# Head of a hybrid layer kernel: the first modulation by single channel blocks, with the products of the high parts first

## The reference, cut to what matters

```python
c_act = silu(c)
mod = c_act @ w_mod + b_mod              # six vectors of 1024
sh_m, sc_m, gt_m, sh_f, sc_f, gt_f = split(mod, 6)
h = rms_norm(x, g_pre_mix) * (1.0 + sc_m) + sh_m
proj = h @ w_in                          # 7 x 1024 columns
b_a, c_a, v_a, x_b, g_b, u_a, u_b = split(proj)
y_a = b_a * conv3(c_a * v_a)
x_b = conv4(x_b)
y_b = rg_lru(x_b) * gelu(g_b)            # two block-diagonal gates, a scan
...                                      # merge, output projection, MLP
```

## Time and profile before

| | us |
|---|---|
| median of 3 runs (lowest to highest) | 826.84 (826.39 to 827.14) |
| the profiled execution | 826.06 |
| its span, first to last instruction | 824.2 |
| TensorE busy | 815.0 (99%) |
| VectorE, ScalarE, GpSimd busy | 507.1, 440.4, 29.1 |

### The profile page before, as it was taken

One profiled execution on the slowest core, in us unless ns is written; L12 is line 12 of the kernel. 1 busy time (PEld: TensorE's weight loads), 2 busy tenths in 40 slices (PEclk: granted clock), 3 DMA queues, 4 the chain that ended last, 5 costly groups with the idle time before them and its releaser, 6 DMA issues.

```text
span 824.2 us, 12511 instructions
## 1 busy us (share of the span) xinstructions
PE 815.0 (99%) x4292; PEld 704.3 (85%) x4292; DVE 507.1 (62%) x672; ACT 440.4 (53%) x655; POOL 29.1 (4%) x30
## 2 busy tenths in 40 slices
PE   8999999999999999999999999999999999999997
PEld 8887888888888888888888899999999888888885
DVE  4776666665585655665784688777776533333335
ACT  6557777776664443444243657666676632233332
POOL 1640000000000000000000000000000000000000
PEclk8999999999999999999999999999999999999999
DMA  9951433326096666676437031333333423322302
GB/s 320 348 159 33 118 109 108 107 78 182 26 271 190 201 188 178 193 204 178 128 127 231 1 103 52 103 102 102 103 109 119 155 103 102 99 82 99 102 1 102
DMA packets 132895, 109.52 MB, mean 133 GB/s; under 512 B 4460, under 2 KB 117252, under 8 KB 132868
## 3 DMA queue, kind: packets, MB, share of 16 engines
q1 hardware_dynamic: 132772, 109.12, 44.3%
q10 hardware_dynamic: 64, 0.02, 0.0%
q0 software_dynamic: 32, 0.02, 0.0%
HBM read 107.04 MB, written 2.10 MB: 132 GB/s over the span
## 4 chain that ended last, share of the span: by engine, by line
PE 94%; DVE 2%; ACT 1%; DMA 1%; issue 1%; SPq 0%; ACTq 0%; DVEq 0%
PE ps L438 31%; PE ps L439 30%; PE ps L440 30%; PE ps L1488 1%; DMA graw<-in_w_gate_i_dram 1%; PE ps L1509 0%; DMA erows<-in_b_mod_dram 0%; PE ps L1653 0%; PE ps L1496 0%; DVE sp L1075 0%; PE ps L1522 0%; DVE w_lo L1143 0%; PE ps L1625 0%; PE ps L1626 0%; PE ps L1535 0%
## 5 line engine op out<-in xcount | busy, mean ns | idle before, releaser
L438 PE MATMUL ps<-ht_hi,w_hi 128*128 128x512 f32 x448 | 175.5, 392 | 0.0
L439 PE MATMUL ps<-ht_lo,w_hi 128*128 128x512 f32 x448 | 174.7, 390 | 0.0
L440 PE MATMUL ps<-ht_hi,w_lo 128*128 128x512 f32 x448 | 174.4, 389 | 0.0
L1051 DVE TENSOR_TENSOR w_lo<-raw,w_hi 128x1024 fp32r<-128x1024 f32 x100 | 121.9, 1223 | 57.0 <-ACT w_hi L653 55.1
L653 ACT ACTIVATE w_hi<-raw 128x1024 fp32r<-128x1024 f32 x96 | 100.4, 1050 | 32.6 <-PE ps L440 30.9
L438 PEld LDWEIGHTS ps<-ht_hi,w_hi 128*128 128x128 f32 x448 | 84.3, 188 | 18.7 <-issue 1.0
L438 PE MATMUL ps<-w_hi,hd_hi 128*128 128x512 f32 x256 | 99.6, 389 | 0.0
L439 PE MATMUL ps<-w_lo,hd_hi 128*128 128x512 f32 x256 | 99.6, 389 | 0.0
L440 PE MATMUL ps<-w_hi,hd_lo 128*128 128x512 f32 x256 | 99.6, 389 | 0.0
L440 PEld LDWEIGHTS ps<-ht_hi,w_lo 128*128 128x128 f32 x448 | 84.3, 188 | 17.8
L439 PEld LDWEIGHTS ps<-ht_lo,w_hi 128*128 128x128 f32 x448 | 84.3, 188 | 17.1
(11 more groups left out here) (234 smaller groups left out, 1504.0 us busy)
## 6 DMA issues: line engine op xcount, KB each, us to landing
raw<-in_w_in_dram SPq DMA_DIRECT2D x48, 512.0 KB, 4.8
modraw<-in_w_mod_dram SPq DMA_DIRECT2D x32, 512.0 KB, 4.0
raw<-in_w_mlp_down_dram SPq DMA_DIRECT2D x32, 512.0 KB, 3.3
up_raw<-in_w_mlp_up_dram SPq DMA_DIRECT2D x56, 256.0 KB, 3.5
mod_raw<-in_w_mod_dram SPq DMA_DIRECT2D x32, 256.0 KB, 7.3
xs<-in_x_dram SPq DMA_DIRECT2D x8, 512.0 KB, 5.7
raw<-in_w_a_out_dram SPq DMA_DIRECT2D x8, 512.0 KB, 5.3
raw<-in_w_b_out_dram SPq DMA_DIRECT2D x8, 512.0 KB, 5.6
```

The source lines that it names most:

```text
L438: nc.tensor.matmul(dst, l_hi, r_hi, start=first, stop=False, skip_group_check=chained)
L439: nc.tensor.matmul(dst, l_hi, r_lo, start=False, stop=False, skip_group_check=chained)
L440: return nc.tensor.matmul(dst, l_lo, r_hi, start=False, stop=last, skip_group_check=chained)
L1051: V.tensor_tensor(w_lo[:, slot, :], raw[:, slot, :], f(w_hi[:, slot, :]), ALU.subtract).then_inc(w_lo_ready, 1)
```

## The change

- The groups of two channel blocks go; all is done for single blocks k. A load of w_mod is 128 KB (two pieces of 128 columns, 512 bytes each, per input channel) instead of 256 KB, and there are 64 instead of 32. A VectorE step has 128x256 elements instead of 128x512, and there are 64 - 8 = 56 instead of 28. For odd blocks row 0 goes to TensorE directly (pe_rows).
- On SyncE, the first units' weights of block k stand behind row 3 of block k; the eight vector loads stand behind row 7 of block 0.
- mod0_columns(k + 1) stands in TensorE's stream within block k: behind the second low-weight product for k > 0, behind the last low-weight product for k = 0. VectorE does accumulate(k) and modulation_columns(k) in turn; for block 1, one step stands ahead of modulation_columns(0) and six behind it.
- VectorE makes the high part of block 0 straight from PSUM; ScalarE makes the float32 form of block 0 after that, and GpSimd all low parts of the input.
- ScalarE copies x for blocks 1 to 5 in two instructions, one for each half of the tokens. TensorE waits for the first copy before it transposes the second half.
- Within a block TensorE does the six high x high products first, then the six with low weights, then the six with the low input. For k = 0 it does so for units 1, 2, 3, 0 and then for 4, 5; the late transposes of channel blocks 6 and 7 stand behind the first four high x high products.
- Of the unread transposes ahead of the products 4 are left of 12, 5 behind the second token block become 4.

The diff, cut:

```diff
-    GROUPS = ((0, 1), (2, 3), (4, 5), (6, 7))
...
+        def pe_rows(g):
+            return PE_ROWS if g == 0 else g % 2
+
+        def direct_count(g, m):
+            return sum(pe_rows(g0) for g0 in range(g)) + m + 1
...
SyncE
-            for m in range(NB):
-                load_mod0(0, m)
-            load_first_units(0)
-            load_vectors(sp_eng, vectors, vrows, NEARLY, vec_in)
-            for g in range(1, len(GROUPS)):
+            for g in range(NB):
                 for m in range(NB):
                     load_mod0(g, m)
-                    if m == 3:
-                        load_first_units(GROUPS[g - 1][1])
-                    if m == 5:
-                        load_first_units(GROUPS[g][0])
-            load_first_units(NB - 1)
+                    if m == NB // 2 - 1:
+                        load_first_units(g)
+                if g == 0:
+                    load_vectors(sp_eng, vectors, vrows, NEARLY, vec_in)
...
ScalarE
-            act.wait_ge(x_tr, X_BANKS)
-            for k in (4, 5, 2):
-                A(xnt[:, k, :], ps[:, k, :], ACT.Copy).then_inc(xnt_ready, 1)
+            def input_copy(half):
+                cs = slice(half * 2 * P, (half + 1) * 2 * P)
+                act.wait_ge(x_tr, half + 1)
+                A(xnt[:, 1:X_BANKS, cs], ps[:, 1:X_BANKS, cs], ACT.Copy).then_inc(xnt_ready, 1)
+
+            input_copy(0)
             first_units_hi(0)
-            for k in GROUPS[0]:
-                modulate(k, 0)
-            act.wait_ge(x_tr, NB)
+            input_copy(1)
+            modulate(0)
...
+            for k in range(1, NB):
+                first_units_hi(k)
...
+                modulate(k)
...
VectorE
-            accumulate(0, range(PE_ROWS, NB))
-            dve.wait_ge(x_tr, X_BANKS)
-            V.tensor_copy(xnt[:, 3, :], ps[:, 3, :]).then_inc(xnt_ready_dve, 1)
+            accumulate(0, range(pe_rows(0), NB))
+            accumulate(1, range(pe_rows(1), 2))
             dve.wait_ge(cols_ready, 2)
             modulation_columns(0)
...
+            dve.wait_ge(col0_ready, 2)
+            V.tensor_scalar(ht_hi[:, 0, :], ps[:, 0, :], s_mix[:, 0:1], mcol[:, 0:1], ALU.mult, ALU.add).then_inc(h_hi, 1)
+            accumulate(1, range(2, NB))
+            modulation_columns(1)
+            for k in range(2, NB):
+                accumulate(k, range(pe_rows(k), NB))
+                modulation_columns(k)
...
TensorE
+            def mod0_columns(k):
+                if k > 0:
+
+                    pe.wait_ge(col0_ready, 2 * k)
+                    if k == 3:
+                        pe.wait_ge(cols_ready, 3)
+                    mod0_direct(k, range(pe_rows(k)))
+                pe.wait_ge(mod0_acc, acc_count(k, NB - 1))
...
+                pe.wait_ge(w0_hi_ready, k + 1)
+                pe.wait_ge(h_hi, k + 1)
+                if k == 0:
+
+                    units = units[1:4] + units[0:1] + units[4:]
+                for some in (units[:4], units[4:]) if k == 0 else (units,):
+                    for i, dst, cs in some:
+                        if k == 0 and i == 0:
+                            pe.wait_ge(h_f32, 1)
+                        if k == 0 and i >= 4:
+                            pe.wait_ge(xnt_ready, i - 1)
+                        nc.tensor.matmul(dst, hi[:, cs], ht_hi[:, k, :], start=k == 0, stop=False)
+                    if k == 0 and len(some) == 4:
+                        for k_late, late in X_LATE.items():
+                            for t in range(TB):
+                                last = input_transposes(k_late, t, late)
+                            last.then_inc(x_tr, 1)
+                    pe.wait_ge(w0_lo_ready, k + 1)
+                    for i, dst, cs in some:
+                        nc.tensor.matmul(dst, lo[:, cs], ht_hi[:, k, :], start=False, stop=False)
+                        if i == (5 if k == 0 else 1) and k < NB - 1:
+                            mod0_columns(k + 1)
+                    pe.wait_ge(h_lo, k + 1)
+                    for i, dst, cs in some:
+                        last = nc.tensor.matmul(dst, hi[:, cs], ht_lo[:, k, :], start=False, stop=k == NB - 1)
```

More of the change, by code:

```diff
@@ L695, in _ @@
                 A(xnt[:, k, :], ps[:, late, :], ACT.Copy).then_inc(xnt_ready, 1)
[L696 to L701, removed]
+            act.wait_ge(xnt_ready, 4)
+            for k in range(1, NB):
+                first_units_hi(k)
+                if k == NB - 1:
                     act.wait_ge(sp_step, 1)
@@ L1098, in accumulate @@
                     else:
                         dve.wait_ge(mod0_acc, acc_count(g, m - 1))
-                        V.scalar_tensor_tensor(mod0[:, :, cs] if m == NB - 1 else acc, part, c_act[:, m:m + 1], acc,
-                                               ALU.mult, ALU.add).then_inc(mod0_acc, 1)
-            def modulation_columns(g):
-                dve.wait_ge(mod0_sum, g + 1)
-                k0, k1 = GROUPS[g][0], GROUPS[g][-1] + 1
-                V.tensor_tensor(mcol[:, k0:k1], ps[:, B_T1, k0:k1], cols[:, C_BS + k0:C_BS + k1], ALU.add).then_inc(col0_ready, 1)
-                for k in GROUPS[g]:
-                    V.scalar_tensor_tensor(s_mix[:, k:k + 1], ps[:, B_T1, NB + k:NB + k + 1], cols[:, C_BC + k:C_BC + k + 1],
-                                           cols[:, C_GX + k:C_GX + k + 1], ALU.add, ALU.mult).then_inc(col0_ready, 1)
+                        V.scalar_tensor_tensor(mod0[:, :, g * P:(g + 1) * P] if m == NB - 1 else acc, mod0_rows_of(r),
+                                               c_act[:, m:m + 1], acc, ALU.mult, ALU.add).then_inc(mod0_acc, 1)
@@ L1111, in _, with modulation_columns @@
+            def modulation_columns(k):
+                dve.wait_ge(mod0_sum, k + 1)
+                V.tensor_tensor(mcol[:, k:k + 1], ps[:, B_T1, k:k + 1], cols[:, C_BS + k:C_BS + k + 1], ALU.add).then_inc(col0_ready, 1)
+                V.scalar_tensor_tensor(s_mix[:, k:k + 1], ps[:, B_T1, NB + k:NB + k + 1], cols[:, C_BC + k:C_BC + k + 1],
+                                       cols[:, C_GX + k:C_GX + k + 1], ALU.add, ALU.mult).then_inc(col0_ready, 1)
             dve.wait_ge(cols_sum, 1)
@@ L1506, in mod0_columns, with input_transposes @@
                                         ident[0:NCOL - NEARLY, 0:NCOL - NEARLY])
-                for k in GROUPS[g]:
-                    for a in range(2):
-                        last = nc.tensor.matmul(ps[:, B_T1, a * NB + k:a * NB + k + 1], mod0[:, a, k * P:(k + 1) * P],
-                                                ones[:, 0:1], start=g > 0, stop=True, skip_group_check=True)
+                for a in range(2):
+                    last = nc.tensor.matmul(ps[:, B_T1, a * NB + k:a * NB + k + 1], mod0[:, a, k * P:(k + 1) * P],
+                                            ones[:, 0:1], start=pe_rows(k) == 0, stop=True, skip_group_check=True)
                 last.then_inc(mod0_sum, 1)
-            last_tokens = ps[:, X_BANKS - 1, (TB - 1) * P:]
+            def input_transposes(k, t, dst):
+                return nc.tensor.transpose(ps[:, dst, t * P:(t + 1) * P], xs[:, t, k * P:(k + 1) * P], ident[:, :])
+            last_tokens = ps[:, 0, (TB - 1) * P:]
             unread(9, last_tokens)
@@ L1538, in _ @@
[L1538 to L1559 removed]
+            pe.wait_ge(xnt_ready, 2)
```

135 lines of the change are left out of this document (50 added, 85 removed).

## The result

| | before | after |
|---|---|---|
| median on the same chip | 826.62 us (825.79 to 827.14, 4 runs) | 833.49 us (831.48 to 834.45, 4 runs) |
| the profiled execution | 826.06 | 833.51 |
| its span | 824.2 | 831.7 |
| TensorE busy | 815.0 (99%) | 815.1 (98%) |

The account below looks back on a forecast made before the run. TensorE, busy 99%, was taken to bound the kernel, VectorE its rounds after the change. Products starting 5.4 us sooner but lasting 43.7 instead of 36.7 gave +1.6, the chain behind +3.2: 831.6 us; forecast 828.5 to 834.5 (0.60), full range 825.0 to 836.5.

Parts of the forecast that it names:

- first product: Start of TensorE's first-layer products once block 0's high part is ready: 16.1 instead of 21.50, 5.4 us gained.
- C(1): Moment TensorE starts block 1's column matmuls: predicted 22.2, between 20.9 at full clock and 23.9 at half clock.
- C(1) to C(7): From block 1's column matmuls to block 7's on TensorE: three rounds of 5.38, three of 4.79, plus 0.4, 30.9 us.
- C(7) to raw0b's second low part: From block 7's column matmuls through VectorE's softplus steps and two raw0b subtractions, one softplus step stretched: 7.65 us.
- gate point: Start of block 1's gate matmuls on TensorE, 81.99 before the change: predicted 4.85 us later.
- way round: Per block, VectorE's last step to TensorE's columns and back to VectorE's next step: 0.77 us besides the steps.
- TensorE alone would need 4.44 a block: TensorE's own work per block in the rounds: 4.09 + 0.35 us, 26.6 in all.
- faster rival: VectorE's 128x256 step under 0.44 us, rounds bound by TensorE at 26.6 instead of 30.9: 825.6 to 824.4; chance 0.13.
- VectorE becomes the bound: In the rounds of single blocks VectorE sets the pace; TensorE waits 0.35 to 0.95 us in each block.
- The loads cost nothing: w_mod loads of 128 KB take 4.8 us a block within a 5.1 us round: costed at nothing, cover 1 to 2 us.
- The order of the products costs 0: High x high products first within a block only moves where low parts are needed and costs no matmul: 0.
- chain behind the products: Waits from raw0b's low parts through gate weights, convolution and sigmoids to TensorE's gate matmuls: no slack, adds 3.2 us.

## Why the prediction was right, and where its sizes were off

The direction held, and so did its ground: the first product came 3.9 us sooner, and single blocks gave it back with more. The size came out low: 4.8 us forecast, 6.9 measured. The first three steps were taken 3.2 us too short together, the last two 0.7 too long. By the steps of the prediction, in the profiled executions:

| step | predicted | measured |
|---|---|---|
| first product | 16.1 (15.7 to 16.5) | 17.62 |
| from there to C(1) | 6.1 | 6.61 |
| C(1) to C(7) | 30.9 | 32.12 |
| C(7) to raw0b's second low part | 7.65 | 7.29 |
| from there to the gate point | 26.09 | 25.78 |
| gate point against 81.99 | +4.85 | +7.43 |

- **First product: wrong by 1.5, outside its bounds.** I let VectorE go straight from its last normalisation (11.60) into the steps. That ended at 12.28, since a block of x came 0.56 us late for ScalarE; then VectorE waited 0.83 for the first row, and 0.59 for row 9, which came near 15.9 and not at 14.5 to 15.3. The high part itself took 0.81 and not 0.70.
- **To C(1): right within 0.5.** I stood between full and half clock; it was at the lower level from about 18 to 21 us. With the clock held up the same stretch ended at 22.82.
- **Step and gap of 128x256: right** (0.48 and 0.593 against 0.484 and 0.59).
- **The way round: mis-sized.** I had 0.77 us from the end of the last step to the next block's first. It is 0.76 to mcol and 0.20 for mcol and s_mix, 0.96. With 4.62 for eight steps and 4.03 for seven that makes 5.58 and 4.99, and the rounds from block 3 on are 5.61, 5.01, 5.59 and 5.01. The row read as "eight" one-column matmuls is four float32 matmuls with two records each, so that one matmul costs what I gave to two. Six times 0.19 is nearly all of the 1.2 us missing in C(1) to C(7).
- **"TensorE alone would need 4.44 a block": wrong, though it did not enter the sum.** It left out the direct rows, and gave the columns 0.35 instead of 0.56. TensorE needs 4.65 and 5.01, 9.66 for two blocks, where the kernel before took 9.3, and not the 9.0 of my sum. Six rounds are 29.0 us, not 26.6. The faster rival rested on the 26.6; even a free VectorE step would have given back some 3 us at most, and it deserved less than its 0.13.
- **VectorE becomes the bound: half right.** It is so into even blocks (5.6 against 4.65); into odd ones TensorE needs the same 5.01. The kernels with two direct rows showed it: with VectorE relieved, TensorE alone took 5.48.
- **The loads cost nothing: wrong at the start, nearly right later.** The rows cost VectorE 2.8 us of waiting up to 20 us, and in the rounds they hide behind the way round; they are the next bound as soon as that is shortened. Here 271 GB/s at a busy share of 0.94 stand against 350 at 1.08 with the larger pieces, 288 against 324 for each full share. By the Trainium skill (DMA: Bandwidth & Descriptors, Specifications) pieces of 512 bytes reach line rate. The measurement differs from that by about a tenth, as the earlier trace rows had suggested. What halving the bytes gave with VectorE one step ahead, 2.3 us between overlapping intervals, says about how near this bound is.
- **The order of the products costs 0: wrong.** 0.8 us alone, in the kernel before. In the changed kernel it lies within the wait for c_sb (0.95) before 64.59. Nor is what follows quite without slack: the copy came 2.1 us later there and the gate point 1.06.
- **The chain behind the products: right**, in its length (25.78 for 26.09) and in the stretched softplus steps (7.29 for 7.65). Of the wait of about 2 us expected at the first gates, 1.27 came there and 1.30 at the second.

Counted on TensorE from the first product to the gate point, the stretch grew by 11.3 us (60.5 to 71.8) against a start 3.9 sooner. Its waits are 1.39, 0.90, some 1.7 at columns and 2.57 at the gates, less 0.51 before: 6.1. The small matmuls are 28 column and 16 direct records for 24 before, at 0.11: 2.2. The late transposes, which stood ahead of the products, are 1.6. The lower clock stretched the products of block 0 by about 1.0, and those of the kernel before by 0.5: 0.5 more. That is 10.4; the rest, 0.9, lies in the products that start about 0.1 late behind each group of small ones and behind each wait, of which there are more now. This sum is worked out from the rows, and no single run shows it.

What stays open: why x and the rows come between 0.5 and 1 us earlier or later from one execution to the next, and how much each of the clock's falls between 24 and 34 us costs; they came in some executions of a kernel and not in others.

## What to carry over

Work that is cut finer to start sooner pays its fixed parts once per piece: here the way round two engines (0.96 us), the one-column matmuls on the engine that bounds the kernel, and smaller transfers. Before counting on the earlier start, work out the steady round for each engine in turn, small instructions included, and compare it with the old round; an early start of a few microseconds is worth nothing if a round of eight grows by half a microsecond. Then ask which wait behind the changed stretch already has no slack: moving two loads and six small steps there in the kernel before gave 0.8 us, and no version with the early start beat the kernel before.

## What the runs showed of the hardware

- One-column float32 matmuls appear as two records each and cost TensorE about 0.11 us a record at full clock, half of a 128x512 product, plus 0.1 for the next product. Moving a row of w_mod from VectorE (0.59) to TensorE costs 0.36 to 0.40 there.
- The granted clock fell to 0.50 near 18 us, behind groups of one-column matmuls and a wait of 1.04, and in several kernels again between 26 and 34 us, behind waits of 0.9 and 1.4. With unread transposes in these waits it stayed at 1.00 in one profiled execution; in two others with them it was at 0.58 and 0.57 from 16 to 20 us, and at 0.50 from 26 to 32 us behind a wait of 3.4. So they are no sure remedy.
- At a busy share of 0.94 the DMA engines moved 271 GB/s with mostly 512-byte pieces, and at 1.08 they moved 350 with larger ones.
- Eight dependent VectorE steps on 128x256 cost 4.74 us where eight on 128x512 cost 6.86: half the elements for 0.69 of the time.
